# A two-layer model and an expert block on one core: the first FFN block reordered, other output blocks taken during attention

## The chip, the cores and the metric

The kernel is one program for one core of a Trainium2 chip. The metric is the device time of one execution in microseconds; of several executions the median is taken. "Before" was measured in three runs, and one execution more was recorded by the hardware profiler.

## What is computed

The reference runs a model of two layers on a sequence of 512 tokens of width 1024, and then one block of another kind on its result. Layer 0 mixes tokens with a gated linear recurrence, layer 1 with stick-breaking attention of 16 heads. Both have the same shape; cut to it:

```python
for layer in range(2):
    h = _rmsnorm(x, norm_mix_g[layer])
    mix = _rglru_mixer(h, ...) if layer == 0 else _sb_mixer(h, ...)   # ends in  y @ w_out
    x = x + mix
    h = _rmsnorm(x, norm_ffn_g[layer])
    x = x + (silu(h @ w_gate) * (h @ w_up)) @ w_down                  # d_ff = 2816
return second_block(_rmsnorm(x, final_g), ...)                        # attentions, 16 experts
```

All is in float32.

## The kernel before

**Layout.** X holds the sequence transposed: 8 chunks c of 128 channels, each of 512 tokens. A float32 product is made of three matmuls, high x high, high x low and low x high, and each operand is kept as its rounded high part and the low rest. For weights, ACT writes the high part (WH<-RAW, L1579) and DVE the low one (WL<-RAW,WH, L1955); for the normed input these are HH and HL.

**Weights.** Each load goes to one of six RAW buffers, from SP's queue. A *unit* is a piece of weights that is split at one time. WH and WL have six half-slots; a unit of 8 tiles takes two, an FFN unit ("st", 4 tiles) one. When PE's program comes to a unit, `ahead` splits the units that fit into the slots behind it (`settle`, `split`).

**One list of steps.** The Order object writes one list; each engine's program walks it and emits its own share. So a step's place in the list sets its place on every engine's queue. `split` is an ACT instruction and a DVE instruction; `split_high` is ACT's alone and `split_low` DVE's.

**The mixer's output.** Output block c of 8 is 8 tiles, 24 matmuls of 512 columns. Then `add_x` (DVE, L2137) adds it to X chunk c, and `normal` makes the FFN's input of it: for c < 4 `pair` and rounding, for c >= 4 the combinations of chunk c - 4 and chunk c (`combine`, `combine_parts`), which are twice the work on DVE. The square of each chunk (ACT) is summed for the norm; chunks 1 to 5 by accumulating DMAs on POOL's queue (`square_in`, SA<-SQ and SA<-SX, L1481), each of which waits for the one before, and chunks 6 and 7 by DVE (`add_square`, L2016). In layer 1, parts of four output blocks (7 of their 8 tiles) are taken as filler work in attention (`sb_order`, `project`), here the even blocks; only the eighth tile of these is left for after attention, as 3 matmuls.

**The FFN.** For each of 22 blocks i of 128 hidden channels, gate and up projections are computed as a 2x2 scheme with seven products (W11, T1, T2, W21, T3, W22, T4) in place of eight, each of 4 tiles, 12 matmuls of 256 columns. Products take rows of HH, or combinations of them held in SH and SO. They need sums of weights: `sum_in` starts two accumulating DMAs on POOL's queue (L1540), `sum` is an addition on DVE (L1550). Between products ACT copies a partial result out of the PSUM bank (`tap` a, d, b, c, L1658), and the next product that adds to the same bank waits for it: T2 for a, W22 for d, T3 for b, T4 for c (W21 for d from block 1 on). The norm's scale is applied to the results alone: block 0 has `root_sums` (PE: 8 small matmuls, L2654; ACT: a table load, a square root of 4 columns, four copies that spread it, L1627 and L1631) and `root_spread` (PE: L2660; ACT: RS, L1636), and `output_b`, `output_a` need RS.

**Block 0** (`ffn_order`, the branch `i == 0`) has an order of its own, in which W21, T1 and T2 are taken in pieces of k as the last chunks come in:

```python
product(W11); tap("a"); normal(o, norm - 1, DC - 1); ahead(W11)
```

After the mixers comes the second block, and at the end 16 experts, whose weights, some 200 MB, are streamed while PE works; the first of these loads waits for a matmul of the stage before.

Of the kernel before, what the change touches and what calls it, by code (L numbers as in the profile page):

```python
# [18 lines left out]
DC = 8  # L19
# [67 lines left out]
class Order:  # L87


    def __init__(self):  # L90
        self.steps, self.units, self.groups = [], [], {}
        self.bank, self.before = {}, {}
        self.free, self.freed = list(range(8)), {}
        self.rounded, self.parted, self.unit_of = set(), set(), {}

    def add(self, *step):
# [57 lines left out]
    def settle(self):  # L154
        self.pos, p = [], 0
        for u in range(len(self.units)):
            p += p % self.size(u)
            self.pos.append(p)
            p += self.size(u)
        steps, self.steps, v = self.steps, [], AHEAD  # L160
        for s in steps:
            if s[0] != "ahead":
                self.steps.append(s)
                continue
            while v < len(self.units) and self.pos[v] + self.size(v) <= self.pos[s[1]] + HALVES:
                self.split(v)
                v += 1

    def split(self, u):
        if u + 2 < len(self.units) and self.units[u + 2][0] == "st" and self.units[u][0] != "st":  # L170
            self.sums(*self.units[u + 2][1])
        name, idx, _ = self.units[u]
        if name != "st":
            if u not in self.parted:
                self.add("split_low" if u in self.rounded else "split", u)
            return
# [213 lines left out]
def ffn_order(o, layer, norm):  # L390
    for half in range(2):
        for f in range(FH):
# [19 lines left out]
            if i == 0:  # L412
# [3 lines left out]
                ahead(W11)  # L416
                o.add("add_square", norm - 1, DC - 2)
                o.add("add_square", norm - 1, DC - 1)
                ahead(W21)
                for k0, k1 in ((0, 2), (2, 3)):  # L420
# [6 lines left out]
                tap("b")  # L427
                for j in (T1, T2, W22):
                    ahead(j)
                product(W22)  # L430
                o.claim("rs", norm - 1)
                o.add("root_sums", norm - 1)
                ahead(T3)
                product(T3)
                tap("c")
            else:
                ahead(W11)
                product(W11)
                if f:
                    o.add("output_a", layer, i - 1)  # L440
# [20 lines left out]
            product(T4)  # L461
            if i == 0:
                o.add("root_spread", norm - 1)
                o.release(("rs", norm - 1), "root", "rs", norm - 1)
            o.add("output_b", layer, i)
            o.release(("B", layer, i), "scaled", "b", layer, i)
        o.add("output_a", layer, i)
# [12 lines left out]
def sb_order(o):  # L480
    def project():
        for c in range(DC):
            for i in range(3):
# [13 lines left out]
                yield from work  # L497
        for c in range(0, DC, 2):
            def done(c=c):
# [45 lines left out]
    for c in range(DC):  # L545
        key = ("out", 1, c)
        if c % 4 == 0:
            u = o.unit("wbo", (slice(c, c + 3, 2), slice(None), DC - 1), 2)
        if c % 2:
            o.lin(key, [("wbo", (c,), 8)], "o")  # L550
        else:
            key = ("out", 1, c, "last")
            o.lin(key, [Part(u, c % 4 // 2, 1, c % 4 == 2)], "o", fresh=c == 0, k0=DC - 1)
        add_x(o, key, c)
# [544 lines left out]
def program(nc, I, OUT, plan, stop=None):  # L1099
    o = whole_order()  # L1100
    S = {}
    with ExitStack() as ctx:
# [457 lines left out]
        def x_ready(e, n, c):  # L1560
            if n == 0:
                e.wait_ge(*d_x[c]())
            else:
                e.wait_ge(*xup(*((None, ("out", 0, c), ("d", 0, 1, c), ("out", 1, c) if c % 2 else ("out", 1, c, "last"),
                                  ("d", 1, 1, c))[n])))
# [1691 lines left out]
```

## Time and profile before

| | us |
|---|---|
| three runs: median (lowest to highest) | 2107.09 (2101.16 to 2112.15) |
| the profiled execution | 2103.63 |
| its span, first to last instruction | 2101.8 |
| PE busy | 2060.8 |
| DVE busy | 1210.4 |
| ACT busy | 903.9 |
| POOL busy | 207.0 |

The profiled execution took 1.8 us more than its span. Busy times of the engines overlap. A matmul is counted from its start to the end of its results, and consecutive ones overlap, so a busy PE says only that it did not stand idle; the distance between starts tells its pace. Idle time of DVE, ACT or POOL costs nothing unless PE waits for what comes after it.

### The profile page before, as it was taken

How to read it: one execution, taken by the hardware profiler on the slowest of the kernel's cores; microseconds unless marked ns; L12 is line 12 of the kernel's file. 1: busy time of each engine (PE TensorE's matmuls, PEld its weight loads, DVE VectorE, ACT ScalarE, POOL GpSimd, SP SyncE). 2: the span in 40 equal slices, each digit the busy share in tenths (PEclk: the TensorE clock that was granted, in tenths of full speed). 3: DMA queues.
4: the chain of work that ended last, by engine and by line, in shares of the span. 5: the costliest groups of instructions: out<-in, count | busy, mean ns of one | idle time of the engine just before them, and what ended most of it. 6: DMA issues, size and time to landing. Idle time of an engine off the chain costs nothing.

```text
span 2101.8 us, 29721 instructions
## 1 busy us (share of the span) xinstructions
PE 2060.8 (98%) x11737; PEld 1570.3 (75%) x11737; DVE 1210.4 (58%) x2038; ACT 903.9 (43%) x1514; POOL 207.0 (10%) x230
## 2 busy tenths in 40 slices
PE   9998999999999989999999999999999999999998
PEld 7878998998777779989988777777787534444443
DVE  7887865876666678847866656565564312122123
ACT  7776643653455556526643556433333110011012
POOL 0221101101000011001110010162100000000000
PEclk9999999999999999999999999999999999999999
DMA  6246846853222257756724322242236999999996
GB/s 220 74 123 157 205 137 158 210 155 122 71 61 66 65 126 196 181 136 179 204 90 144 102 68 71 66 97 68 67 113 257 395 427 426 427 426 427 427 426 269
DMA packets 116617, 401.18 MB, mean 191 GB/s; under 512 B 12544, under 2 KB 27136, under 8 KB 92928
## 3 DMA queue, kind: packets, MB, share of 16 engines
q1 hardware_dynamic: 97392, 365.55, 48.0%
q0 software_dynamic: 16304, 28.32, 8.6%
q10 hardware_dynamic: 2784, 5.41, 0.7%
q8 instruction: 95, 1.56, 0.3%
q14 instruction: 42, 0.34, 0.1%
HBM read 393.20 MB, written 2.10 MB: 188 GB/s over the span
## 4 chain that ended last, share of the span: by engine, by line
PE 82%; DVE 7%; DMA 5%; ACT 3%; issue 2%; ACTq 0%; POOL 0%; SPq 0%; DVEq 0%; POOLq 0%
PE PS L2564 12%; PE PS L2566 11%; PE PS L2565 11%; PE PS L3017 8%; PE PS L2598 7%; PE PS L2599 7%; PE PS L2600 7%; PE PS L3059 4%; DMA SL<-in_wgu_dram 4%; PE PS L2636 2%; DVE WL L1955 1%; PE PS L2727 1%; PE PS L3001 1%; PE PS L2751 1%; PE PS L2741 1%
## 5 line engine op out<-in xcount | busy, mean ns | idle before, releaser
L1955 DVE TENSOR_TENSOR WL<-RAW,WH 128x512 fp32r<-128x512 f32 (+4 forms) x522 | 445.6, 856 | 223.9 <-ACT WH L1579 218.3
L1579 ACT ACTIVATE WH<-RAW 128x512 fp32r<-128x512 f32 (+4 forms) x522 | 385.1, 743 | 287.6 <-PE PS L2566 145.1
L2564 PE MATMUL PS<-HH,WH 128*128 128x512 f32 x688 | 278.4, 405 | 1.8 <-issue 0.8
L2566 PE MATMUL PS<-HH,WL 128*128 128x512 f32 x688 | 268.6, 390 | 0.0
L2565 PE MATMUL PS<-HL,WH 128*128 128x512 f32 x688 | 268.0, 390 | 0.0
L3017 PE MATMUL PS<-SL,XS 128*64 128x512 f32 x928 | 220.6, 595 | 4.9 <-DMA SL<-in_wgu_dram 4.5
L2598 PE MATMUL PS<-HH,WH 128*128 128x256 f32 x704 | 202.3, 287 | 6.8 <-issue 4.0
L2600 PE MATMUL PS<-HH,WL 128*128 128x256 f32 x704 | 200.3, 285 | 0.0
L2599 PE MATMUL PS<-HL,WH 128*128 128x256 f32 x704 | 200.3, 284 | 0.0
L3017 PEld LDWEIGHTS PS<-SL,XS 128*64 128x64 f32 x928 | 70.2, 137 | 133.7 <-issue 131.6
L2598 PE MATMUL PS<-SH,WH 128*128 128x256 f32 x528 | 151.0, 286 | 7.8 <-DVE WL L1955 5.3
L2564 PEld LDWEIGHTS PS<-HH,WH 128*128 128x128 f32 x688 | 129.2, 188 | 39.1 <-issue 11.0
L2600 PE MATMUL PS<-SH,WL 128*128 128x256 f32 x528 | 150.4, 285 | 0.0
L2599 PE MATMUL PS<-SO,WH 128*128 128x256 f32 x528 | 150.4, 285 | 0.0
L2566 PEld LDWEIGHTS PS<-HH,WL 128*128 128x128 f32 x688 | 129.1, 188 | 28.2
L2565 PEld LDWEIGHTS PS<-HL,WH 128*128 128x128 f32 x688 | 129.4, 188 | 25.2 <-issue 0.5
L2598 PEld LDWEIGHTS PS<-HH,WH 128*128 128x128 f32 x704 | 136.1, 193 | 9.6 <-issue 6.1
L2564 PE MATMUL PS<-MH,WH 128*128 128x512 f32 x352 | 137.0, 389 | 0.0
L2565 PE MATMUL PS<-ML,WH 128*128 128x512 f32 x352 | 137.0, 389 | 0.0
L2566 PE MATMUL PS<-MH,WL 128*128 128x512 f32 x352 | 136.9, 389 | 0.0
L2599 PEld LDWEIGHTS PS<-HL,WH 128*128 128x128 f32 x704 | 136.1, 193 | 0.9 <-issue 0.8
L2600 PEld LDWEIGHTS PS<-HH,WL 128*128 128x128 f32 x704 | 136.2, 193 | 0.0
(432 smaller groups left out, 3647.2 us busy)
## 6 DMA issues: line engine op xcount, KB each, us to landing
SL<-in_wgu_dram SPq DMA_DIRECT2D x115, 1024.0 KB, 20.5
SL<-in_wdn_dram SPq DMA_DIRECT2D x52, 1024.0 KB, 23.3
RAW<-in_w_dram SPq DMA_DIRECT2D x46, 512.0 KB, 3.6
RAW<-in_wu_dram SPq DMA_DIRECT2D x44, 512.0 KB, 4.4
RAW<-in_wg_dram SPq DMA_DIRECT2D x44, 512.0 KB, 6.0
RAW<-in_wd_dram SPq DMA_DIRECT2D x32, 384.0 KB, 3.1
RAW<-in_wqkv_dram SPq DMA_DIRECT2D x24, 512.0 KB, 3.6
RAW<-in_wu_dram SPq DMA_DIRECT2D x44, 256.0 KB, 3.2
```

What stands on the lines that cost most here:

```text
L1579: e.activation(split_slot(WH, u)[:, 0:n], unscaled(u), ACT.Copy).then_inc(*whs.did("u", u))
L1955: e.tensor_tensor(wl, unscaled(u), wh.bitcast(F), ALU.subtract).then_inc(*wlo.did("u", u))
L2564: e.matmul(out, wh[:, w], xh, start=k == 0, stop=False)
L2565: e.matmul(out, wh[:, w], xl, start=False, stop=False)
L2566: m = e.matmul(out, wl[:, w], xh, start=False, stop=k == g.total - 1)
L2598: e.matmul(out, wh[:, w], xh, start=opens and k == 0, stop=False, skip_group_check=True)
L2599: e.matmul(out, wh[:, w], xl, start=False, stop=False, skip_group_check=True)
L2600: m = e.matmul(out, wl[:, w], xh, start=False, stop=k == 3, skip_group_check=True)
L2636: m = e.transpose(bank(*key)[:, 128 * j:128 * j + 128], src, ident)
L2727: e.matmul(heads_bank(p)[:, f:f + n], QK[z][r, 0, 128 * i:128 * i + 128], QK[z][r, 1, 0:n], start=i != 0, stop=False, skip_group_check=True)
L3017: m = e.matmul(bank("h", i, n)[64 * e2:64 * e2 + 64, :], XS[:, k, x0:x0 + 64], SL[slot(l0 + e2)][:, 512 * n:512 * n + 512], start=k == 0, ...
L3059: m = e.matmul(bank("y", i, n)[64 * e2:64 * e2 + 64, :], HT[k // 2][:, 2 * (k % 2) + f, 64 * e2:64 * e2 + 64], SL[slot(l0 + e2)][:, 1024 * ...
```

## The change

1. `split` looks four units ahead in place of two for the first FFN unit, so the two `sum_in` DMAs of block 0 (and of the first block of the second half) are issued two units earlier.
2. For output weights 5, 6 and 7 of both mixers the low part is no longer made with the high part, but behind the next `add_x`.
3. Block 0 of the FFN: T4's split and `add_square` come after T2 and taps d and b; `root_sums` comes after T3 and tap c, not before T3; `root_spread` and `output_b` of block 0 come after block 1's W11.
4. In layer 1 the blocks taken during attention are 0, 1, 2, 3. Their last tiles are one unit of four tiles, where there were two units of two; blocks 4 to 7 are whole.

```diff
@@ -92,6 +92,7 @@
         self.bank, self.before = {}, {}
         self.free, self.freed = list(range(8)), {}
         self.rounded, self.parted, self.unit_of = set(), set(), {}
+        self.later = []
 
     def add(self, *step):
         self.steps.append(step)
@@ -161,15 +162,24 @@
         for s in steps:
             if s[0] != "ahead":
                 self.steps.append(s)
+                if s[0] == "add_x":
+                    for u in self.later:
+                        self.add("split_low", u)
+                    self.later = []
                 continue
             while v < len(self.units) and self.pos[v] + self.size(v) <= self.pos[s[1]] + HALVES:
                 self.split(v)
                 v += 1
 
     def split(self, u):
-        if u + 2 < len(self.units) and self.units[u + 2][0] == "st" and self.units[u][0] != "st":
-            self.sums(*self.units[u + 2][1])
+        if u + 4 < len(self.units) and self.units[u + 4][0] == "st" and self.units[u][0] != "st":
+            self.sums(*self.units[u + 4][1])
         name, idx, _ = self.units[u]
+        if (name, idx) in (("wout", (5,)), ("wout", (6,)), ("wout", (7,)), ("wbo", (5,)), ("wbo", (6,)),
+                           ("wbo", (7,))):
+            self.add("split_high", u)
+            self.later.append(u)
+            return
         if name != "st":
             if u not in self.parted:
                 self.add("split_low" if u in self.rounded else "split", u)
@@ -414,9 +424,6 @@
                 tap("a")
                 normal(o, norm - 1, DC - 1)
                 ahead(W11)
-                o.add("add_square", norm - 1, DC - 2)
-                o.add("add_square", norm - 1, DC - 1)
-                ahead(W21)
                 for k0, k1 in ((0, 2), (2, 3)):
                     for j in (W21, T1, T2):
                         product(j, k0, k1)
@@ -425,17 +432,26 @@
                 tap("d")
                 product(T2, 3, 4)
                 tap("b")
-                for j in (T1, T2, W22):
-                    ahead(j)
+                ahead(W21)
+                o.add("add_square", norm - 1, DC - 2)
+                o.add("add_square", norm - 1, DC - 1)
+                ahead(T1)
+                ahead(T2)
                 product(W22)
+                ahead(W22)
+                product(T3)
+                tap("c")
                 o.claim("rs", norm - 1)
                 o.add("root_sums", norm - 1)
                 ahead(T3)
-                product(T3)
-                tap("c")
             else:
                 ahead(W11)
                 product(W11)
+                if i == 1:
+                    o.add("root_spread", norm - 1)
+                    o.release(("rs", norm - 1), "root", "rs", norm - 1)
+                    o.add("output_b", layer, 0)
+                    o.release(("B", layer, 0), "scaled", "b", layer, 0)
                 if f:
                     o.add("output_a", layer, i - 1)
                     o.release(("A", layer, i - 1), "scaled", "a", layer, i - 1)
@@ -459,11 +475,9 @@
                 late("low_f")
             ahead(T4)
             product(T4)
-            if i == 0:
-                o.add("root_spread", norm - 1)
-                o.release(("rs", norm - 1), "root", "rs", norm - 1)
-            o.add("output_b", layer, i)
-            o.release(("B", layer, i), "scaled", "b", layer, i)
+            if i:
+                o.add("output_b", layer, i)
+                o.release(("B", layer, i), "scaled", "b", layer, i)
         o.add("output_a", layer, i)
         o.release(("A", layer, i), "scaled", "a", layer, i)
         for what in ("silu_f", "mul_f", "high_f", "low_f"):
@@ -495,7 +509,7 @@
                     natural(c - 1)
                 yield
                 yield from work
-        for c in range(0, DC, 2):
+        for c in range(4):
             def done(c=c):
                 add_x(o, ("out", 1, c), c)
 
@@ -544,13 +558,13 @@
     o.only(0, 1, 2, 3, 4, 5, 6, 7)
     for c in range(DC):
         key = ("out", 1, c)
-        if c % 4 == 0:
-            u = o.unit("wbo", (slice(c, c + 3, 2), slice(None), DC - 1), 2)
-        if c % 2:
+        if c == 0:
+            u = o.unit("wbo", (slice(0, 4), slice(None), DC - 1), 4)
+        if c < 4:
+            key = ("out", 1, c, "last")
+            o.lin(key, [Part(u, c, 1, c == 3)], "o", fresh=c == 0, k0=DC - 1)
+        else:
             o.lin(key, [("wbo", (c,), 8)], "o")
-        else:
-            key = ("out", 1, c, "last")
-            o.lin(key, [Part(u, c % 4 // 2, 1, c % 4 == 2)], "o", fresh=c == 0, k0=DC - 1)
         add_x(o, key, c)
         if c < DC - 1:
             normal(o, 3, c)
@@ -1561,7 +1575,7 @@
             if n == 0:
                 e.wait_ge(*d_x[c]())
             else:
-                e.wait_ge(*xup(*((None, ("out", 0, c), ("d", 0, 1, c), ("out", 1, c) if c % 2 else ("out", 1, c, "last"),
+                e.wait_ge(*xup(*((None, ("out", 0, c), ("d", 0, 1, c), ("out", 1, c) if c > 3 else ("out", 1, c, "last"),
                                   ("d", 1, 1, c))[n])))
 
         def act_split(e, u):
```

**What it moves, POOL's queue at the end of layer 0's mixer.** L1540 are the accumulating DMAs of the weight sums (L1554 in the changed kernel), L1481 (L1495) those of the squares. Before:

```order
L1481 DMA SA<-SQ 128x512 x2
L1481 DMA SA<-SX 128x512
L1540 DMA RAW<-in_wg_dram 128x512
L1540 DMA RAW<-in_wu_dram 128x512
L1481 DMA SA<-SX 128x512 x2
L1540 DMA RAW<-in_wg_dram 128x512
```

After:

```order
L1554 DMA RAW<-in_wg_dram 128x512
L1554 DMA RAW<-in_wu_dram 128x512
L1495 DMA SA<-SQ 128x512 x2
L1495 DMA SA<-SX 128x512 x3
L1554 DMA RAW<-in_wg_dram 128x512
L1554 DMA RAW<-in_wu_dram 128x512
```

The two sums of block 0 stand ahead of all five squares, where three squares were ahead of them.

**ACT's queue in layer 0's first FFN block,** from the square of the last chunk. S<-PS is tap d, the first U<-PS tap b, the second tap c, G<-PS tap a of block 1. Before:

```order
L1584 ACTIVATE SX<-X 128x512
L1579 ACTIVATE WH<-RAW 128x512 x3
L1658 ACTIVATE S<-PS 128x256
L1658 ACTIVATE U<-PS 128x256
L1579 ACTIVATE WH<-RAW 128x512 x3
L1627 ACT_TABLE_LOAD
L1627 ACTIVATE SM<-PS,V 128x4
L1631 ACTIVATE ST<-C,SM 128x128 x4
L1579 ACTIVATE WH<-RAW 128x512
L1658 ACTIVATE U<-PS 128x256
L1579 ACTIVATE WH<-RAW 128x512
L1636 ACTIVATE RS<-PS 128x512
```

After:

```order
L1598 ACTIVATE SX<-X 128x512
L1593 ACTIVATE WH<-RAW 128x512 x2
L1672 ACTIVATE S<-PS 128x256
L1672 ACTIVATE U<-PS 128x256
L1593 ACTIVATE WH<-RAW 128x512 x4
L1672 ACTIVATE U<-PS 128x256
L1641 ACT_TABLE_LOAD
L1641 ACTIVATE SM<-PS,V 128x4
L1645 ACTIVATE ST<-C,SM 128x128 x4
L1593 ACTIVATE WH<-RAW 128x512 x3
L1650 ACTIVATE RS<-PS 128x512
```

One rounding moves behind taps d and b, and tap c moves ahead of the table load and the four copies; RS has three roundings between it and the copies, before it had two and tap c.

**DVE's queue at layer 1's output blocks,** from the add of block 3 on (SO is the low part of a combination). Before:

```order
L2137 TENSOR_TENSOR X<-X,PS 128x512
L2028 SCALAR_TENSOR_TENSOR SO<-S,SH 128x256
L2010 SCALAR_TENSOR_TENSOR S<-X,NG,S 128x256
L1998 SCALAR_TENSOR_TENSOR HL<-X,V,HH 128x256
L1955 TENSOR_TENSOR WL<-RAW,WH 128x1024
L2137 TENSOR_TENSOR X<-X,PS 128x512
L2028 SCALAR_TENSOR_TENSOR SO<-S,SH 128x256
```

After:

```order
L2151 TENSOR_TENSOR X<-X,PS 128x512
L2042 SCALAR_TENSOR_TENSOR SO<-S,SH 128x256
L2024 SCALAR_TENSOR_TENSOR S<-X,NG,S 128x256
L2012 SCALAR_TENSOR_TENSOR HL<-X,V,HH 128x256
L2151 TENSOR_TENSOR X<-X,PS 128x512
L1969 TENSOR_TENSOR WL<-RAW,WH 128x1024
L2042 SCALAR_TENSOR_TENSOR SO<-S,SH 128x256
```

Before, a low part of weights (WL) stands between the rows of chunk 3 and the add of block 4; after, the add of block 4 is ahead of it.

## Rows read from the trace of the kernel before

**Rows 1.** The page, part 1

```profile
PE 2060.8 (98%) x11737; PEld 1570.3 (75%) x11737; DVE 1210.4 (58%) x2038; ACT 903.9 (43%) x1514; POOL 207.0 (10%) x230
```

**Rows 2.** View of waits, PE, 130 to 200 us: who waited for whom, total, times, longest

```profile
PE PS L2598 <- DVE WL L1955: 3.1, 2, 1.9
```

**Rows 3.** View of waits, PE, 700 to 800 us

```profile
PE PS L2598 <- DVE WL L1955: 4.4, 2, 3.4
PE PS L2598 <- issue: 3.4, 1, 3.4
```

**Rows 4.** Timeline of PE, layer 0: start, length, ..., idle before and its releaser

```profile
165.78 0.28 PE L2598 MATMUL PS<-HH,WH 128*128 128x256 f32 x1
...
169.98 0.38 PE L2598 MATMUL PS<-SH,WH 128*128 128x256 f32 x1 [1.89 <-DVE WL L1955]
...
176.29 0.36 PE L2598 MATMUL PS<-HH,WH 128*128 128x256 f32 x1 [1.23 <-DVE WL L1955]
...
187.64 0.28 PE L2598 MATMUL PS<-SH,WH 128*128 128x256 f32 x1
...
189.08 0.28 PE L2598 MATMUL PS<-SH,WH 128*128 128x256 f32 x1
...
193.48 0.36 PE L2598 MATMUL PS<-SH,WH 128*128 128x256 f32 x1 [1.06 <-ACT U L1658]
```

**Rows 5.** Timeline of PE, layer 1

```profile
751.96 0.50 PE L2564 MATMUL PS<-OH,WH 128*128 128x512 f32 x1 [1.24 <-DVE WL L1955]
...
763.66 0.28 PE L2598 MATMUL PS<-HH,WH 128*128 128x256 f32 x1
...
769.39 0.39 PE L2598 MATMUL PS<-SH,WH 128*128 128x256 f32 x1 [3.42 <-DVE WL L1955]
...
775.70 0.35 PE L2598 MATMUL PS<-HH,WH 128*128 128x256 f32 x1 [0.96 <-DVE WL L1955]
...
777.20 0.95 PE L2654 MATMUL PS<-C,SA 128*128 128x1 f32 x8
...
794.05 0.36 PE L2598 MATMUL PS<-SH,WH 128*128 128x256 f32 x1 [1.06 <-ACT U L1658]
```

**Rows 6.** Stretches: length, busy us (count) by engine, PE's granted clock, DMA share, GB/s

```profile
165.00:195.00 30.00, 24.44 (x160) 22.41 (x159) 22.73 (x41) 19.96 (x39) 5.25 (x6) 0.89 0.60 132
...
1800.00:2000.00 200.00, 197.41 (x1036) 89.18 (x1032) 39.04 (x64) 19.41 (x31) 0.00 (x0) 1.00 1.01 427
```

**Rows 7.** Timeline of DVE, both layers

```profile
164.51 0.69 DVE L1550 TENSOR_TENSOR RAW<-RAW 128x512 f32<-128x512 f32 x1 [3.31 <-DMA RAW<-in_wu_dram]
...
165.72 0.68 DVE L2137 TENSOR_TENSOR X<-X,PS 128x512 f32<-128x512 f32 x1
...
761.63 0.68 DVE L2137 TENSOR_TENSOR X<-X,PS 128x512 f32<-128x512 f32 x1
```

**Rows 8.** The chain that ended last, 120 to 200 us: start, length, what

```profile
155.07 9.41 DMA RAW<-in_wu_dram
...
185.52 0.87 PE PS L2660 x2
```

**Rows 9.** Timeline of ACT, layer 0

```profile
179.09 0.63 ACT L1579 ACTIVATE WH<-RAW 128x512 fp32r<-128x512 f32 x1 [1.59 <-DVE RAW L1550]
179.74 1.28 ACT L1627 ACT_TABLE_LOAD   x1
181.04 0.27 ACT L1627 ACTIVATE SM<-PS,V 128x4 f32<-128x4 f32 x1
181.55 1.28 ACT L1631 ACTIVATE ST<-C,SM 128x128 f32<-128x128 f32 x4 [0.25 <-DVE SM L2020]
```

**Rows 10.** ACT's taps, all: duration ns min/median/max, first and last start

```profile
L1658 ACT ACTIVATE U<-PS x88: 360/373/385, 176.1 to 1057.7; 128x256 f32<-128x256 f32 x88
```

**Rows 11.** View of the tile SX: DVE's adds; landing of the squares' DMAs

```profile
L2016 DVE TENSOR_TENSOR SA<-SA,SX x4: 682/688/693, 175.8 to 776.0; 128x512 f32<-128x512 f32 x4
...
DMA to landing us min/median/max: 3.2/4.2/8.2
```

## The prediction, made before the change was run

> **What bounds the kernel now.** The page's first part comes first: PE is busy for 2060.8 us of a span of 2101.8 [rows 1], so nearly every microsecond not spent on matmuls is a wait of PE, and only those waits can be won. The view of PE's waits by stretch says where they are. Layer 0's mixer end and first FFN block has 3.1 us of waiting for low weights (WL) ahead of the products' matmuls (L2598), and some smaller ones [rows 2]; the same place of layer 1 has 4.4 us for WL and one wait of 3.4 us put down to "issue" [rows 3]. These are the two places that the change touches.
>
> A product is 12 matmuls and takes 1.44 us (187.64 to 189.08) [rows 4]: one matmul per 0.12 us. An output block of the mixer is 24 matmuls of 0.227 us, 5.44 us, worked out from two starts in layer 1: from 751.96 to 763.66 lie two whole blocks and one of 3 matmuls, 51 x 0.229 = 11.7 us [rows 5]. In layer 0 the products start at 165.78, and from there to the T3 of block 1 lie 11 products, 15.84 us; they take until 193.48, that is 27.7 us [rows 4]. In layer 1 it is 763.66 to 794.05, 30.4 us [rows 5]. So 11.9 and 14.6 us are lost, part idle, part clock: the mean granted clock from 165 to 195 us is 0.89 [rows 6], which between the two levels of 1.2 and 2.4 GHz means 6.6 of 30 us at the lower.
>
> **What is late, layer 0.** Matmuls of T1 start at 169.98 after 1.89 us of waiting for WL [rows 4]. On DVE that WL stands behind the work on output block 6, whose add starts at 165.72, though PE had finished block 6 at 165.78 - 5.44 = 160.34. DVE had been held for 3.31 us by an accumulating DMA of a weight sum [rows 7], which took 9.41 us from its issue at 155.07 [rows 8]. **Layer 1.** No DMA is late there. The even blocks need only 3 matmuls after attention, so PE gives DVE two blocks almost at once, and the second half of the blocks costs DVE the most: block 5 was complete on PE at 763.66 - 5.44 - 0.68 = 757.54, its add starts at 761.63 [rows 7]. DVE is 4.1 us behind, and PE stops for 3.42 us at 769.39. An earlier wait of 1.24 us at 751.96 is a WL queued behind the same work [rows 5].
>
> **The tail of block 0, both layers.** W22 needs the copy ("tap") d of a finished product. ACT has ahead of it the rounding of unit T4, which waits for a DVE sum; W22 waits 0.96 us in layer 1 [rows 5]. T4 needs tap c, which stands behind root_sums' work on ACT: a table load of 1.28 us, begun at 179.74, then four copies that start at 181.55 and take 1.28 us [rows 9]. That is the 3.4 us under "issue" [rows 3]: PE waited for nothing but ACT.
>
> **The change, part by part.** No matmul is added or removed. One load, one rounding and one low part of two tiles go (two such units become one of four tiles); they cost no path, as they stand in attention under PE's matmuls.
>
> *A, layer 0 up to W22: 4.7 us.* The weight sums are issued two units earlier, before the squares. They land 10 us before DVE asks, so the 3.31 us go. DVE's add of block 6 comes at 162.3 at the latest, 3.4 earlier; everything to the last low of block 7, 8.3 us by the timeline, keeps its length, and ends at 170.6. PE gets to it at 165.78 + 3.5 x 1.44 = 170.8, so PE sets the time: W22 starts at 165.78 + 4 x 1.44 = 171.6 in place of 176.29 [rows 4].
> The row shows 9.41 us for that DMA [rows 8]. The Trainium skill (DMA: Bandwidth & Descriptors, section on the anatomy of a DMA on the SWDGE path) fits 2.0 us plus bytes at 436 GB/s, an estimate of 2.6 us for 256 KB: by that rule the sum would land before DVE asks even now, and part A would come to nothing; the trace disagrees with it here.
>
> *B, layer 0 from W22 (time u) to block 1's T3: 2.0 us.* Taps d and b no longer stand behind T4's rounding. Tap b runs u+0.2 to 0.6 (0.38 us each [rows 10]), T4's rounding to 1.15, its WL (0.6 us steps) to 1.75, two adds of 0.69 [rows 11] to 3.2. The root_sums matmuls, now behind T3, take 0.8 at the full clock [rows 5]: 3.3 to 4.15. DVE makes a WL and the next sum by 4.4; ACT's fourth rounding waits for it, as it does now for 1.59 us [rows 9], and ends at 5.0. Tap c ends at 5.4, so T4 starts at 5.5: 1.3 us of the wait stay. T4 and W11 end at 8.4. Meanwhile ACT does the table (6.65), the small root, and the copies (8.55); root_spread follows, 0.87 us [rows 8], so T1 starts at 9.5. Then ACT has three roundings, the spread's copy (10.7), tap a, the rounding of T4 behind a DVE sum (12.1), tap d, one rounding, the silu table and silu (14.8) and tap b (15.15): T3 at u+15.2. Now it is 193.48 - 176.29 = 17.2 [rows 4].
>
> *C, layer 1 up to W22: 7.7 us.* Blocks 0 to 3 take 3 matmuls each, then blocks 4 to 7 take 5.44 each: PE's sum is the same, so W11 starts at 763.66 less the 1.24 wait = 762.3. DVE starts block 4 late, about 747.6, but needs 4.9 us per block (add 0.6, a WL of 1.15, 3.1 of parts) against 5.44 on PE, and is down to its own chain's end at block 7: add at 763.5, last low at 767.0. PE gets there at 762.3 + 5.0 = 767.3. W22 starts at 768.0 in place of 775.70 [rows 5]. The margin is 0.3 us; a low weight moved behind an add is still 1.4 to 2.2 us ahead of PE.
>
> *D, layer 1 from W22 on: 3.1 us.* u+15.2 against 794.05 - 775.70 = 18.3 [rows 5].
>
> *Cost at nothing.* The add ahead of the low part of wout and wbo 5 to 7 is covered by the block of 5.44 us that PE has before it needs that weight. The last stage is bound by HBM traffic, DMA share 1.01 at 427 GB/s [rows 6], but its loads start behind the compute before them, so it moves as a whole and gives nothing back.
>
> Sum: 4.7 + 2.0 + 7.7 + 3.1 = 17.5 us. **Ends.** Upwards, both waits left in each tail (1.3 and about 1.2 us) could vanish too: 22.4. Downwards, B and D could be nothing and C half: 8.5. Against the profiled execution, 2103.63 - 17.5 = 2086.1; it stands 3.5 us under the median of the runs shown, so in their terms 2107.09 - 17.5 = **2089.6 us**.
> The ACT row after a table load starts 0.02 us behind its 1.28 us in these rows [rows 9]; the Trainium skill (ScalarE: Activation LUTs, what a table load costs) has 1.38 us of draining on top. By that figure root_spread comes about 1.4 us later in each layer, and the sum would be about 14.8; the trace decides for 17.5.
>
> **The rivals.** *The clock keeps its dips.* What fell before was a stretch after PE had idled; W11 to W22 now run without a gap, but u+2.9 to u+5.5 is still thin (small matmuls, a wait). If 6.6 us a layer stay at half speed, with layer 1 taken like layer 0, 3.3 a layer are kept and 17.5 - 6.6 = 10.9 won: 2096.2. *DVE stays the bound in layer 1,* since its margin is 0.3 us and it starts block 4 late: C is lost, 9.8 remain: 2097.3. For it: 4.1 us of lag now. Against it: 0.5 us regained in each of four blocks. *Slower, by the POOL queue.* The squares of the norm go as five accumulating DMAs, each waiting for the one before, and now stand behind the sums. DVE needs the last at u+1.75. From 145.8 that allows 27.5 us, 5.5 per link; landing is 3.2 to 8.2 us, median 4.2 [rows 11]. If every link took 9.41 as the sum's DMA did, the last would land at 192.8 and 790.4, 19.5 and 20.7 us late, giving -17.5 + 40.2 = +22.7: 2129.8. It decides from 5.5 us a link, and turns the sign from about 7.2. Against it: the sums are now out of the way before the first square. *It does nothing,* the waits passing to T3 and T4 whole: 2107.
>
> **How the numbers follow.** A measurement of this kernel can tell about 0.5% (10.5 us) from no change. The forecast has 0.65; the clock 0.15; DVE in layer 1 0.12; nothing 0.03; slower 0.05. The first two are faster: 0.80. The next two lie within 0.5%: 0.15. Slower 0.05. The range goes from 2083 (the upper end of the gain and some scatter of the runs) to 2102 (past both partial cases), leaving out the last two cases (0.08) and about as much on the edges of the others.
>
> **What would show it.** DVE without a DMA wait before its add of block 6 in layer 0; PE with no wait between W11 and W22 in either layer; T4 of block 0 waiting about 1.3 us, not 3.4; granted clock near 1.0 from 165 to 175 and 762 to 770; from W11's start to block 1's T3 about 21 us in each layer. Wrong would be: a WL or HL wait inside the first three products of layer 1, root_sums waiting for a square, or the sum of PE's waits unchanged.

## The result and the profile after

The changed kernel takes **2088.0 us** (median of five runs, 2085.37 to 2094.58) against 2107.09 before (by now five runs, with the same median). The ratio is 0.9917, its 95% interval [0.9897, 0.9937]: 0.8% faster, beyond the 0.5% that the prediction set as its bound. Forecast were 2089.6 us and a range of 2083 to 2102. The profiled execution took 2085.37 us (its span is 2083.6), 18.3 us less than the profiled one of before, where the sum said 17.5. The interval is 4 us wide to each side, so the medians can't tell 17.5 us from 16 or 20; what each part brought is read from the profiles.

Line numbers behind the edit are 14 higher than before. Part 1 of the page, after, against [rows 1]:

```profile
PE 2052.6 (99%) x11737; PEld 1564.3 (75%) x11737; DVE 1208.8 (58%) x2037; ACT 903.8 (43%) x1513; POOL 207.6 (10%) x230
```

PE is busy 8.2 us less, with the same matmuls. Part of what had counted as busy was matmuls at half the clock: before, the granted clock was 0.50 from 176.5 for 6.8 us, and from 770.4 and 784.1 for 3.4 us each; after, in neither place.

The view of PE's waits, after, 130 to 200 us, against [rows 2]:

```profile
PE PS L2612 <- ACT U L1672: 1.1, 1, 1.1
PE PS L2612 <- DVE WL L1969: 1.1, 1, 1.1
PE PS L2578 <- DVE WL L1969: 1.0, 1, 1.0
PE PS L2612 <- issue: 0.2, 1, 0.2
```

The same for 700 to 800 us, against [rows 3]:

```profile
PE PS L2612 <- ACT U L1672: 1.1, 1, 1.1
PE PS L2612 <- DVE WL L1969: 1.1, 1, 1.1
PE PS L2612 <- issue: 0.2, 1, 0.2
PE PS L2612 <- DVE HL L2066: 0.2, 1, 0.2
```

All that made up the 3.1 and 4.4 us for WL, and the 3.4 us under "issue", is gone. Two waits stay in each layer, 1.1 us each, where the prediction had 1.3 and about 1.2: at T4 and, for tap b, at T3 of block 1. The row of T4 names WL, but tap c sets it: tap c ends at 177.21 and T4 starts at 177.31, and where tap c is moved ahead (below) T4 waits for nothing. The 1.0 us under L2578 is ahead of an output block of the mixer and was there before. New are 0.2 us under "issue" in each layer and 0.2 us for HL in layer 1.

Timeline of PE, after, layer 0: W11, W22, root_sums, T4, and T3 of block 1, against [rows 4]:

```profile
166.04 0.28 PE L2612 MATMUL PS<-HH,WH 128*128 128x256 f32 x1
...
172.17 0.36 PE L2612 MATMUL PS<-HH,WH 128*128 128x256 f32 x1 [0.22 <-issue]
...
175.22 1.02 PE L2668 MATMUL PS<-C,SA 128*128 128x1 f32 x8
177.31 0.36 PE L2612 MATMUL PS<-HH,WH 128*128 128x256 f32 x1 [1.07 <-DVE WL L1969]
...
187.17 0.36 PE L2612 MATMUL PS<-SH,WH 128*128 128x256 f32 x1 [1.07 <-ACT U L1672]
```

Layer 1, against [rows 5]: W11, the last piece of T1, W22, T4, and T3 of block 1:

```profile
755.44 0.28 PE L2612 MATMUL PS<-HH,WH 128*128 128x256 f32 x1
...
760.81 0.39 PE L2612 MATMUL PS<-SH,WH 128*128 128x256 f32 x1 [0.18 <-DVE HL L2066]
...
762.02 0.36 PE L2612 MATMUL PS<-HH,WH 128*128 128x256 f32 x1 [0.23 <-issue]
...
767.15 0.36 PE L2612 MATMUL PS<-HH,WH 128*128 128x256 f32 x1 [1.07 <-DVE WL L1969]
...
777.02 0.35 PE L2612 MATMUL PS<-SH,WH 128*128 128x256 f32 x1 [1.08 <-ACT U L1672]
```

From W11 to block 1's T3 it is 21.1 and 21.6 us (27.7 and 30.4 before; forecast 21). In layer 0 W22 starts 6.13 us after W11 (10.5 before), in layer 1 6.58 us (12.0 before); from W22 to T3 it is 15.00 us in both.

Stretches, after, against [rows 6]; the last figures are the granted clock, the DMA share and GB/s:

```profile
165.00:195.00 30.00, 27.62 (x213) 26.09 (x212) 24.10 (x45) 20.43 (x42) 6.10 (x7) 1.00 0.75 173
765.00:800.00 35.00, 32.84 (x263) 31.73 (x262) 27.75 (x52) 24.78 (x50) 6.08 (x7) 1.00 0.77 196
```

The clock is full (1.00) through both places. Before, it was 0.89 in the first.

Timeline of DVE, after, against [rows 7]: the add of block 6 in layer 0, two adds of squares, and the add of block 7 in layer 1:

```profile
161.71 0.68 DVE L2151 TENSOR_TENSOR X<-X,PS 128x512 f32<-128x512 f32 x1
...
173.59 1.48 DVE L2030 TENSOR_TENSOR SA<-SA,SX 128x512 f32<-128x512 f32 x2
...
757.17 0.68 DVE L2151 TENSOR_TENSOR X<-X,PS 128x512 f32<-128x512 f32 x1
```

The add of block 6 comes at 161.71, 4.0 us earlier than before, and DVE waits for no DMA there or at the squares.

### The profile page after: what moved, and what is told of

It is laid out like the page before. It is cut to its first block, busy times and chain, and to the rows that moved or that the text cites. A ratio compares the mean times of both kernels' runs of the same rounds, so it can differ in the third digit from the quotient of the medians.

```text
span 2083.6 us, 29717 instructions
## 1 busy us (share of the span) xinstructions
PE 2052.6 (99%) x11737; PEld 1564.3 (75%) x11737; DVE 1208.8 (58%) x2037; ACT 903.8 (43%) x1513; POOL 207.6 (10%) x230
## 4 chain that ended last, share of the span: by engine, by line
PE 86%; DVE 6%; DMA 3%; ACT 3%; issue 2%; ACTq 0%; SPq 0%; POOL 0%; DVEq 0%; POOLq 0%
PE PS L2578 12%; PE PS L2580 12%; PE PS L2579 12%; PE PS L3031 9%; PE PS L2612 7%; PE PS L2614 7%; PE PS L2613 7%; PE PS L3073 4%; DMA SL<-in_wgu_dram 3%; PE PS L2650 2%; DVE WL L1969 1%; PE PS L2741 1%; PE PS L3015 1%; PE PS L2765 1%; PE PS L2755 1%
## 5 line engine op out<-in xcount | busy, mean ns | idle before, releaser
L2578 PE MATMUL PS<-HH,WH 128*128 128x512 f32 x688 | 278.4, 405 | 2.5 <-issue 0.8
L2578 PEld LDWEIGHTS PS<-HH,WH 128*128 128x128 f32 x688 | 129.2, 188 | 39.8 <-issue 11.0
L2578 PE MATMUL PS<-MH,WH 128*128 128x512 f32 x352 | 137.0, 389 | 0.0
```

Source lines behind the costliest of these rows:

```text
L2578: e.matmul(out, wh[:, w], xh, start=k == 0, stop=False)
```

## The experiments

Each kernel here is the one before with one change made alone, or the changed kernel with one change taken out or something added. "Stage 0" is the time from the first matmul of the mixer's output blocks in layer 0 (at 120.5 us before) to block 1's T3, "stage 1" the same in layer 1, both from PE's timeline of each kernel's one profile. They hold both places, and nothing of the scatter elsewhere. The column after them is their sum against before. Changes are numbered as in the list ahead of the diff. "The tail" is W22 to block 1's T3. Times are in us. Change 2 was not run alone.

| kernel | stage 0 | stage 1 | sum against before | ratio to before, 95% interval |
|---|---|---|---|---|
| before | 73.01 | 86.16 | | |
| changed | 66.49 | 75.86 | -16.8 | 0.9917 [0.9897, 0.9937] |
| 1 alone (a_sums) | 69.47 | 86.43 | -3.3 | 0.9992 [0.9982, 1.0002] |
| 3 alone (b_block0) | 69.98 | 83.47 | -5.7 | 0.9963 [0.9951, 0.9976] |
| 4 alone (c_blocks) | 73.48 | 82.13 | -3.6 | 0.9981 [0.9971, 0.9990] |
| all but 1 (e_sums_late) | 68.73 | 81.20 | -9.2 | 0.9940 [0.9927, 0.9952] |
| all but 2 (d_low_first) | 66.81 | 77.96 | -14.4 | 0.9937 [0.9924, 0.9951] |
| all but 3 (m_old_tail) | 71.37 | 80.49 | -7.3 | 0.9962 [0.9950, 0.9974] |
| all but 4 (l_even) | 66.90 | 81.20 | -11.1 | 0.9947 [0.9934, 0.9960] |
| changed, sixth link (i_six_links) | 65.63 | 75.22 | -18.3 | 0.9909 [0.9896, 0.9922] |
| changed, tap b (g_tap_b) | 65.27 | 74.58 | -19.3 | 0.9922 [0.9904, 0.9939] |
| changed, taps b, c (h_both) | 64.99 | 74.30 | -19.9 | 0.9909 [0.9897, 0.9922] |
| three taps (k_taps) | 64.98 | 74.33 | -19.9 | 0.9913 [0.9901, 0.9926] |
| three taps, sixth link (j_taps_six) | 64.32 | 73.66 | -21.2 | 0.9921 [0.9908, 0.9934] |

**1 alone.** The edit is the lookahead of four units in place of two.

> The kernel before with the earlier weight sums alone. My theory (term A): the accumulating DMAs of block 0's sums no longer hold DVE for 3.31 us ahead of its add of output block 6 in layer 0; W11 to W22 shrinks there from 10.5 us to about 6, and layer 1 stays as it is (12.0 us, and 30.4 from W11 to block 1's T3). The tail of layer 0, W22 to block 1's T3, was 17.2 us; with W22 earlier it should be bound by ACT as in layer 1, so 17.2 to 18.3. Net 3.3 to 4.5 us less than before, ratio 0.9979 to 0.9984. Rival 1, the transfer is hidden anyway by the POOL chain of squares: 0. Rival 2, the squares of the norm come late behind the sums: layer 0's tail longer than 18.3 us and root_sums waits for a square; no gain or a loss.

In stage 0 W22 comes 7.1 us after W11 instead of 10.5, the tail from W22 on is 17.1 us. Stage 1 did not move. The two stages are 3.3 us shorter, the least that was expected, so the DMA was not hidden anyway; and the tail is not above 18.3 us, so the squares were not late. W22 did not come to 6 us, because its own wait of 1.2 us stayed. The row names WL for it, but on ACT tap d ends 0.1 us before W22 starts. By the runs' time the gain can't be told from nothing.

**3 alone.** `ffn_order` of the changed kernel.

> The kernel before with the reordered tail of block 0 alone (both layers). My theory (B and D): W22 to block 1's T3 goes to about 15.2 us in both layers, from 17.2 and 18.3; the waits ahead of W22 stay (W22 starts about 10.5 us after W11 in layer 0 and about 12 in layer 1), except for the 0.96 us wait for tap d in layer 1. Net 5 to 6 us, ratio about 0.9974. Rival, the clock: PE idles for 1.9 us and 3.4 us ahead of the tail as it did, so the stretches at the lower clock stay, and the tail is 1.7 us or more above 15.2 in each layer; net 1.5 to 3 us.

The tails are 15.4 us in both layers, against 15.0 in the changed kernel, and PE did idle ahead of them (1.7 us in layer 0, 4.4 in layer 1). A stretch of this kernel's layer 0 behind the start of T4:

```profile
180.00:184.00 4.00, 3.92 (x20) 3.95 (x21) 0.98 (x3) 3.74 (x8) 0.87 (x1) 0.57 0.93 222
```

The clock is 0.57 for 4 us in the tail, and still the tail is only 0.4 us longer. In the runs below the same 15.4 is found in each tail of this order that holds such a dip (layer 0 of "all but 2" and "all but 4", layer 1 of "all but 1"), and 15.0 in the three that hold none. So a dip costs 0.4 us in this order; the rival's 1.7 us or more is not seen, as PE's lost time mostly falls into waits that ACT sets.

In the old order a dip could cost more, which neither the expectation nor the prediction had. There the time from T4 to block 1's W11 is 1.96 us at the full clock ("1 alone", layer 0) and 3.61 at half ("all but 3", layer 0):

```profile
180.16:182.12 1.96, 1.96 (x15) 1.72 (x15) 1.05 (x2) 0.42 (x1) 0.00 (x0) 1.00 1.05 203
```

```profile
180.23:183.84 3.61, 3.61 (x14) 3.09 (x15) 1.05 (x2) 0.42 (x1) 0.00 (x0) 0.50 0.57 115
```

The whole tail in the old order is 17.1 us where the clock stays full ("1 alone", layer 0), 17.2 where 6.8 us of half clock lie ahead of T4, under the waits for ACT (before, layer 0), and 18.2 to 19.1 where the clock falls at T4, behind the wait of 3.4 us (the other six of this order). What a dip costs hangs on what it falls on.

**4 alone.**

> The kernel before with blocks 0 to 3 in place of the even ones taken during attention, and nothing else. My theory (C): in layer 1 the waits of 1.24 and 3.42 us for low weights go, W11 to W22 shrinks from 12.0 us to about 5.7 to 6.7, layer 0 is unchanged, and the tail of layer 1 stays at about 18.3. Net 7.7 us, ratio 0.9963. Rival, DVE stays the bound: it has the same work, starts block 4 late, and here also has the low part of each weight ahead of the add; then PE still waits for WL or HL in W21 to T2, W11 to W22 stays over 8 us, net 1.2 to 5 us.

W22 comes 9.7 us after W11, with waits for WL and HL in between; stage 1 is 4.0 us shorter, not 7.7. This is the rival's picture. Stage 0, which the edit does not touch, came out 0.5 us longer: W22 came 1.5 us sooner after W11, and the tail took 1.9 us more, with the clock at half from T4 on. So much one profile can differ from another in the old order.

**All but 2.** The special case for output weights 5 to 7 taken out of `split`.

> The changed kernel with the low parts of output weights 5 to 7 back ahead of the adds. My theory (cost and gain of that part at nothing): the same time as the changed kernel within 1 us, profiled 2085.4, ratio 0.991 to before. Rival: DVE's margin in layer 1 (0.18 us of waiting for HL already) is too thin, an add that comes 1.2 us later delays the last chunk, and W11 to W22 grows from 6.6 to 7.8 us in layer 1, with a wait for HL or WL inside it; 1 to 2.5 us slower than the changed kernel.

Stage 1 is 2.1 us longer and W11 to W22 is 8.7 us, so the theory fell. The rival had 7.8 us and 1 to 2.5 us in all; the median is 5 us above that of the changed kernel, but the two intervals overlap. In stage 0 W22 is as early as in the changed kernel. The timeline of DVE at block 4 in layer 1, with the low part first:

```profile
742.05 0.48 DVE L2007 SCALAR_TENSOR_TENSOR HL<-X,V,HH 128x256 fp32r<-128x256 f32 x1
743.52 1.23 DVE L1964 TENSOR_TENSOR WL<-RAW,WH 128x1024 fp32r<-128x1024 f32 x1 [0.98 <-ACT WH L1588]
744.66 0.68 DVE L2146 TENSOR_TENSOR X<-X,PS 128x512 f32<-128x512 f32 x1
```

The changed kernel, the add first:

```profile
740.76 0.68 DVE L2151 TENSOR_TENSOR X<-X,PS 128x512 f32<-128x512 f32 x1
741.83 1.23 DVE L1969 TENSOR_TENSOR WL<-RAW,WH 128x1024 fp32r<-128x1024 f32 x1 [0.39 <-ACT WH L1593]
```

The low part waits for ACT's rounding (0.98 us), and the add, whose data was there, stands behind it. With the add first, DVE idles for 0.39 us there. The same happens at two other places, and together DVE idles 2.25 us around these weights where it idles 0.39 in the changed kernel: 1.9 of the 2.1 us.

**All but 1.**

```diff
-        if u + 4 < len(self.units) and self.units[u + 4][0] == "st" and self.units[u][0] != "st":
-            self.sums(*self.units[u + 4][1])
+        if u + 2 < len(self.units) and self.units[u + 2][0] == "st" and self.units[u][0] != "st":
+            self.sums(*self.units[u + 2][1])
```

> The changed kernel with the weight sums issued as late as before (two units ahead, not four). My theory (A): layer 0 alone loses, by about 4.4 us: W11 to W22 there goes from 6.1 back to about 10.5 us, with a DMA wait of about 3 us on DVE; its tail stays near 15.0; about 2089.8 profiled. In layer 1 DVE was never held by that DMA, so W11 to W22 stays at 6.6. Rival, the clock: idling ahead of the tail brings back a stretch at the lower clock in it, so layer 0's tail grows by up to 1.7 us more, total about +6. Rival, the wait is absorbed by other waits: under +1.

Layer 0 loses 2.2 us, half of what was expected, with DVE's wait of 3.1 us back and the tail at 15.0. The surprise is layer 1, which loses 5.3, though no DMA was late there before. DVE's timeline there:

```profile
756.32 0.69 DVE L1969 TENSOR_TENSOR WL<-RAW,WH 128x512 fp32r<-128x512 f32 x1
761.65 0.69 DVE L1564 TENSOR_TENSOR RAW<-RAW 128x512 f32<-128x512 f32 x1 [4.64 <-DMA RAW<-in_wu_dram]
```

POOL's: the sum's DMA, and two links of the squares behind it:

```profile
751.73 1.58 POOL L1554 DMA_DIRECT2D RAW<-in_wu_dram  x1
754.41 0.86 POOL L1495 DMA_DIRECT2D SA<-SX  x1 [1.11 <-DMA SA<-SX]
763.50 0.86 POOL L1495 DMA_DIRECT2D SA<-SX  x1 [8.22 <-DMA SA<-SX]
```

Issued at 751.73, the sum is there at 761.65, 9.9 us later, and the next link of the squares is issued only 9.1 us after the one before. In the kernel of before the same DMA was issued at 753.20, took at most 7.1 us and so had landed by 760.3, and DVE, which was late, came to it at 760.43, just behind. Once DVE is early (here it was free at 757.0), the DMA is the bound. With 7.1 us for it DVE would still have waited 1.8 us, an estimate; the rest of the 4.64 is this DMA's own 9.9 us. This profile is the slowest of its six runs, 4.3 us over their median, so the 5.3 us are more than a typical execution loses by this. How much more was not shown.

**All but 4.** Back to `range(0, DC, 2)` and the two units of two tiles.

> The changed kernel with the even output blocks taken during attention again, so all parts but that one. My theory (C hangs on the choice of blocks): the 1.24 us wait among the output blocks and one of 3 to 4.5 us for low weights in T1 come back in layer 1, W11 to W22 is 11 to 12 us there instead of 6.6, the tail stays near 15.0 to 15.4; layer 0 as in the changed kernel (21.1 us from W11 to block 1's T3). Net +5.5 to +6.7 us against the changed kernel, about 2094. Rival, suggested by the run without the early sums: in layer 1 the early sums and the moved low parts bring most of it and the choice of blocks little; then +1 to +3 us.

Layer 1 is 5.3 us longer, W11 to W22 is 10.4 us. The view of waits, PE, 730 to 800 us:

```profile
PE PS L2612 <- DVE WL L1969: 3.8, 2, 2.7
PE PS L2578 <- DVE WL L1969: 1.2, 1, 1.2
```

The waits of 1.2 and 2.7 us are those of before [rows 3, 5], the second one smaller; the rest of the 3.8 is T4's. The theory holds, a little under its size; the rival's +1 to +3 us is out.

**All but 3.** The old branch `i == 0`.

> The changed kernel with the old order of block 0 (root_sums ahead of T3, copies d and b behind the rounding), so all parts but that one. My theory (B and D are the order of ACT, not the clock): W22 to block 1's T3 is 18.4 us in both layers instead of 15.0, with T4 waiting 3.4 us, though PE does not idle before W22 by more than 1.2 us; a wait of about 1 us for low weights ahead of W22 in both layers; net +8 to +9 us, about 2096. Rival, the clock: without idling of PE ahead of the tail it keeps full speed, and the tail is 17 us or less; net +4 to +6 us.

The tails are 19.1 and 18.6 us, each with the wait of before ahead of T4. View of waits, PE, layer 0:

```profile
PE PS L2608 <- issue: 3.4, 1, 3.4
PE PS L2608 <- DVE WL L1965: 1.0, 1, 1.0
```

The 1.0 us is ahead of W22. The rival falls: PE had idled for no more than 1.2 us ahead of these tails, and they are not 17 us or less. The theory holds in part. The order of ACT's work makes the wait of 3.4 us, but only 2.1 us of the excess over 15.0 are its own, by the tail of 17.1 us at the full clock in "1 alone"; the other 1.6 to 2.1 us are the clock, which fell to half inside the tail, at T4 (shown above).

**The sixth link.** The square of chunk 6 goes by DMA too:

```diff
-    if 0 < c < DC - 2:
+    if 0 < c < DC - 1:
         o.add("square_in", n, c)
...
-                o.add("add_square", norm - 1, DC - 2)
```

> The changed kernel with the square of chunk 6 also added by an accumulating DMA, a sixth link of the chain, in place of a DVE addition. It asks how near the rival of the POOL queue is. In layer 0 the fifth link is issued at 166.9 and DVE needs the squares at 173.6. My theory: the links keep 3.2 to 5.9 us each, the sixth is issued near 170.2 and lands at 173.5 to 176; DVE has one addition of 0.7 us less; block 0's T4 waits 0.4 to 3 us instead of 1.07 in layer 0, while layer 1, where the fifth link is issued 9.8 us before it is needed, gains up to 0.6 us; net -1 to +2 us. The rival's mechanism (links of 7 us and more on this queue) would show as a wait of 5 us or more for the sixth link in layer 0, net +4 us or more.

POOL's timeline, layer 0, the issues of links five and six:

```profile
162.57 0.85 POOL L1494 DMA_DIRECT2D SA<-SX  x1 [3.32 <-DMA SA<-SX]
...
166.33 0.86 POOL L1494 DMA_DIRECT2D SA<-SX  x1 [1.12 <-DMA SA<-SX]
```

DVE's timeline, its only addition of a square:

```profile
173.25 0.68 DVE L2029 TENSOR_TENSOR SA<-SA,SX 128x512 f32<-128x512 f32 x1
```

The sixth link was issued at 166.33, four us sooner than expected, took 6.4 us and landed at 172.7; DVE did not wait. So the rival's mechanism, links of 7 us and more one after the other, is not there, but the margin was 0.5 us. In the changed kernel itself the five links of layer 0 took 4.8, 5.1, 5.9, 3.2 and 3.5 us; the last landed at 170.4, for a use at 173.59. That is 3.2 us of margin, or 0.6 us a link. The stages are 0.9 and 0.6 us shorter; the median is the same.

**Taps b and c moved.** Tap b of block 1 is put ahead of `silu_f`; in the second kernel tap c of block 0 also ahead of the rounding:

```diff
                 product(W22)
-                ahead(W22)
                 product(T3)
                 tap("c")
+                ahead(W22)
```

> The changed kernel with block 1's copy b put ahead of the silu of block 0 on ACT, so that it no longer stands behind that table load. My theory: the 1.07 us that block 1's T3 waits in each layer go, as the copy can run 1.9 us earlier; net -2.1 us, ratio to the changed kernel 0.9990; the silu is 0.4 us later and nobody waits for it. Rival: the copy waits for T2's matmuls or the next weights come late instead, and the wait only changes its name: 0.

> The changed kernel with that, and also block 0's copy c ahead of the rounding that waits for a DVE sum. My theory: T4 of block 0 starts about 1.1 us earlier in both layers and waits for nothing; but the spread of the root behind it is bound by ACT (table load, root, four copies), whose start moves by only 0.3 to 0.4 us, so PE waits there instead for up to 0.8 us; with copy b the tail goes from 15.0 to 13.5 to 13.9 us per layer, net -2.2 to -3 us against the changed kernel, about 2083 profiled. Rival: the ACT chain decides alone and copy c brings nothing on top of copy b: -2.1. Rival, the clock: the shorter wait changes nothing in it, full either way.

By the stages both theories are right (2.5 and 3.1 us less than the changed kernel), but the profiled executions took 2087.31 and 2087.23 us, not less than its 2085.37. The stages end at block 1's T3. PE's timeline of the second kernel: the spread of the root, and then, behind the stage's end, T4 of block 1:

```profile
180.14 1.12 PE L2677 MATMUL PS<-ST,C 128*128 128x512 f32 x2 [0.87 <-ACT ST L1648]
...
189.74 0.36 PE L2615 MATMUL PS<-HH,WH 128*128 128x256 f32 x1 [0.97 <-ACT U L1675]
```

The first wait, 0.87 us, was expected (up to 0.8). The second, 0.97 us for tap c, has taken the place of that for tap b. From the mixer's first output matmul to the down projection, layer 0 takes 161.66 us in the changed kernel, 161.67 with tap b moved and 161.39 with both. In layer 1 it is 171.02, 170.98 and 171.55 us. So the first rival is right of tap b: the wait only changed its name.

**Three taps, and all.** Tap c of block 1 is moved ahead of `high_f` too; the other kernel has the sixth link besides.

> The changed kernel with three of ACT's copies moved ahead of other work: block 0's copy c ahead of a rounding, block 1's copy b ahead of the silu, and (new against the run before) block 1's copy c ahead of the rounding of the silu's product, where the wait of 0.97 us had gone. My theory: the three waits of 1.07, 1.07 and 0.97 us go, and 0.87 us of waiting for the root's spread stays; from block 0's W22 to block 1's T3 13.5 us as in that run, and no wait at block 1's T4; 1.2 to 1.5 us less per layer than the changed kernel, net -2.4 to -3 us, about 2085.3 in the median. Rival: the wait moves on once more, to the weights' roundings that are now later on ACT; 0 to -1 us.

> That kernel and the sixth accumulating DMA in place of one DVE addition. My theory: DVE comes 0.6 us sooner to the sum that ACT's rounding ahead of the root's table load waits for, so the 0.87 us wait for the root's spread shrinks to about 0.2 to 0.3 in layer 1, and likewise in layer 0 where the sixth link lands in time; W22 to block 1's T3 is 12.9 to 13.1 us; 1.2 us less than without the sixth link, net about -4 us against the changed kernel, about 2084. Rival: with PE asking for the squares 1 us sooner the sixth link is late in layer 0, which gives the gain back there: -3 us.

With three taps moved the wait moves on once more, to a tap of block 2 and not, as the rival had it, to the weights' roundings. View of waits, PE, layer 0:

```profile
PE PS L2680 <- ACT ST L1651: 0.9, 1, 0.9
...
PE PS L2618 <- ACT S L1678: 0.9, 1, 0.9
```

It is now a tap d of block 2 (ACT S). With the sixth link the tails are 12.9 and 12.8 us, as expected, and the stages are 4.4 us shorter than the changed kernel's. Yet the medians are 2088.0 and 2088.3 us, where about 2085.3 and 2084 were expected, and the ratios 0.9913 and 0.9921. None of the five kernels beyond the changed one can be told from it by its time.

## Why the prediction was right, and where its reasons were not

| step | forecast | measured, profile to profile |
|---|---|---|
| A, layer 0 up to W22 | 4.7 | 4.3 |
| B, layer 0, W22 to block 1's T3 | 2.0 | 2.2 |
| C, layer 1 up to W22 | 7.7 | 7.0 |
| D, layer 1, the tail | 3.1 | 3.4 |
| sum | 17.5 | 16.8 |

A and C are differences of the time from the mixer's first output matmul to W22. The other 1.4 us between the two profiles lie outside the two places, 1.1 of it in the experts' stage, which the change does not touch. That the total came so near is in part luck: A and C fell short by 1.1 us, B and D were 0.5 us over, and what stands below on C and D shows two sizes met for reasons that were not the ones given.

**A** was short by one thing, in both layers: W22 was taken to follow without a gap. Tap d begins only when T1's last piece is done, and T2's last piece, 3 matmuls, covers 0.36 us; PE waits 0.22 and needs about 0.4 us more than its pace. That the sums' DMA held DVE is shown by both runs on it. It was not all of A: alone the earlier sums brought W22 3.4 us nearer to W11, and the new order of the taps alone 1.2 us, the wait of 1.23 us ahead of W22 [rows 4], which the prediction counted under A without naming tap d for it. The Trainium skill (DMA: Bandwidth & Descriptors, the anatomy of a DMA on the SWDGE path) would give 2.6 us for it, an estimate; the 9.41 us of [rows 8] and the 9.9 us above disagree, and moving the DMA paid.

**B and D** hold within 0.3 us, and the new tail came as worked out. ACT's timeline after, layer 0, against [rows 9]:

```profile
176.31 0.63 ACT L1593 ACTIVATE WH<-RAW 128x512 fp32r<-128x512 f32 x1 [1.76 <-DVE RAW L1564]
176.84 0.37 ACT L1672 ACTIVATE U<-PS 128x256 f32<-128x256 f32 x1
177.23 1.28 ACT L1641 ACT_TABLE_LOAD   x1
178.52 0.26 ACT L1641 ACTIVATE SM<-PS,V 128x4 f32<-128x4 f32 x1
179.03 1.28 ACT L1645 ACTIVATE ST<-C,SM 128x128 f32<-128x128 f32 x4 [0.24 <-DVE SM L2034]
...
181.78 0.57 ACT L1650 ACTIVATE RS<-PS 128x512 f32<-128x512 f32 x1
```

The fourth rounding still waits for DVE's sum (1.76 us), tap c follows at once, and the table load stands behind it. The next activation starts 0.01 us after the 1.28 us, and the spread of the root at 180.36, 8.2 us after W22 (forecast 8.55). The 1.38 us of draining that the Trainium skill has (ScalarE: Activation LUTs, what a table load costs) is not seen.

What was incomplete is the old side of D. The prediction took 18.3 us for the old tail of layer 1 and laid its length to ACT's order. At the full clock the old order's tail is 17.1 us, so the order is worth 2.1 us in either layer, and the other 1.3 of D's 3.4 us are the clock at half from 784.1 us, behind the wait of 3.4. Both went together, as the wait did. The 17.1 us stand on one tail ("1 alone", layer 0), with 17.2 in layer 0 of before beside it.

**C** came to its size, but not by the step that the prediction named. It said of layer 1 "No DMA is late there", gave the early sums to layer 0 alone and the whole 7.7 us to the choice of blocks, and put the moved low parts under "cost at nothing". The choice of blocks alone brings 4.0 us. Taken out of the full change, the choice is worth 5.3 us in layer 1, the early sums up to 5.3 and the low parts 2.1, and the order of the taps 1.0 us of the way from W11 to W22: each takes away a wait that would otherwise be next, so these don't add up. That C came near 7.7 is luck in this sense: parts that it had priced at nothing there stood in the same change. The low parts were argued as covered on PE; what counted was DVE, on which the add stood behind a wait for ACT. The margin of 0.3 us was used up: the add of block 7 starts 1.7 us after W11, forecast 1.2, and PE waits 0.18 us for HL. The prediction had called a HL wait there a sign that it was wrong; it is one of 0.18 us, and there is none for WL before T4.

**The rivals.** The clock was priced at 3.3 us a layer kept; a dip of 3.4 us in the new tail costs 0.4 us, and in the old order one of 6.8 us cost between nothing (0.1) and 2.1 us, by where it fell. DVE as the bound in layer 1 is what the runs without one of changes 1, 2 and 4 show, and it was right to give it a chance: any one of them missing brings it. The POOL queue was no bound in the changed kernel or with a sixth link, but it was nearer than its chance of 0.05 and the words "out of the way" say: its links averaged 4.9 us in layer 0 of the changed kernel, against the 5.5 from which it decides, and with six links 0.5 us were left. "It does nothing" did not come about.

## What to carry to other kernels

When a wait is taken away, ask of every DMA and every queued instruction near it whether it was in time only because the waiting engine was late; parts that look worth nothing alone may carry the gain together. An add whose data is there should not stand behind an operation that waits for another engine. And a stretch in which one engine sets several waits is judged by its far end: three copies moved on ACT shortened the part that was looked at by 3 us, and the kernel by nothing that could be measured. Last, a stretch at half clock has no fixed price: where other engines set the waits it was nearly free, and where PE's own matmuls set the pace it cost up to 1.6 of its 3.4 us. One profile of a kernel can hold either.

## What was not expected of the hardware

**The sum's DMAs scatter, and with them the kernel.** In the rest of the FFN, which no change touches, DVE waited for these DMAs 0.6 us in the profile of the changed kernel from 795 to 1110 us:

```profile
DVE RAW L1564 <- DMA RAW<-in_wu_dram: 0.6, 1, 0.6
```

In that of "all but 2" 5.7 us, and there PE waited for a tap behind them (the two longest at 966 and 998 us):

```profile
DVE RAW L1559 <- DMA RAW<-in_wu_dram: 5.7, 3, 2.7
```

```profile
PE PS L2607 <- ACT U L1667: 3.4, 3, 1.8
```

Such waits stand in different blocks in different profiles: PE had one of 1.8 to 2.1 us from 260 us (k_taps), 263 (e_sums_late), 964 ("all but 2"), 974 (a_sums), 981 (m_old_tail) and 1030 (i_six_links), each behind a wait of DVE for such a DMA of 2.3 to 3.0 us. In the profiles of before and of the changed kernel there is none. They are likely a part of the spread of the runs, and a reason why 3 us of the stages do not show in the medians; only one execution of each kernel was profiled, so this is argued, not shown.

**The clock falls behind a single wait of 2 us, but not always.** Of these six waits five are followed within 4 us by 3.4 us at half clock (262.5, 266.3, 977.3, 984.7 and 1033.1 us), the one at 964 is not. And in layer 0 of "all but 2" and "all but 4" the clock fell for 3.4 us at 177.6 and 178.6 us, behind waits of 0.2 and 1.07 us that the changed kernel has too, where it did not fall. What decides between the two is open; it was not tried.
